# Seventeen homes for weight units and gathers of 192 one-hot columns in a grouped mixture of experts

## The reference, cut to what matters

```python
scores = sigmoid(t @ router_w)                 # t: (384, 1024), 16 experts
best = argmax(sum of the two best of each group of 4)   # group-limited
top_idx = top_k(where(mask, biased, -inf), 2); top_w normalised
g = einsum("nd,edf->nef", t, w_gate)           # (16, 1024, 1024) weights
u = einsum("nd,edf->nef", t, w_up)
a = silu(g) * u * combine
y = einsum("nef,efd->nd", a, w_down)
x = x + g2 * y                                  # then the final RMSNorm
```

## Time and profile before

| what | value |
|---|---|
| median of three runs (lowest, highest) | 836.02 us (828.83, 836.41) |
| profiled execution | 833.07 us |
| span of its instructions | 831.4 us |
| TensorE, matmul records | busy 746.8 us, 90% of the span |
| TensorE, weight loads | 412.1 us, 50% |
| VectorE | 311.8 us, 38% |
| ScalarE | 187.1 us, 22% |
| GpSimd | 43.3 us, 5% |
| moved by DMA | 261.05 MB, mean 314 GB/s |
| mean granted clock of TensorE | 0.948 |

### The profile page before, as it was taken

The page is one execution under the profiler, slowest core; times in us unless marked ns, Lnnn a source line. Parts: engine busy times, 40 slices in busy tenths (PEclk is TensorE's granted clock), DMA queues, the critical chain, the costliest instruction groups (busy, mean ns, idle before and its releaser), DMA issues.

```text
span 831.4 us, 22823 instructions
## 1 busy us (share of the span) xinstructions
PE 746.8 (90%) x9748; PEld 412.1 (50%) x9749; DVE 311.8 (38%) x802; ACT 187.1 (22%) x392; POOL 43.3 (5%) x102
## 2 busy tenths in 40 slices
PE   5699986788999988999998999999999999999862
PEld 5345553474644466553552654554544554555232
DVE  3898969997012266211210121211201211121138
ACT  3555340200022133021211122201201112221132
POOL 2000100000010001200000000000000000000000
PEclk9989999957999976999999999999999999999985
DMA  8910369820139992699999999999999999999981
GB/s 340 413 43 2 127 247 410 344 97 7 50 119 334 361 364 95 214 406 410 410 410 411 409 411 411 410 410 411 410 409 379 413 411 410 410 410 410 410 334 76
DMA packets 70027, 261.05 MB, mean 314 GB/s; under 512 B 10540, under 2 KB 10588, under 8 KB 65880
## 3 DMA queue, kind: packets, MB, share of 16 engines
q1 hardware_dynamic: 67832, 257.17, 78.5%
q0 software_dynamic: 1552, 2.99, 0.9%
q10 hardware_dynamic: 592, 0.14, 0.1%
HBM read 252.49 MB, written 9.17 MB: 315 GB/s over the span
## 4 chain that ended last, share of the span: by engine, by line
PE 59%; DVE 10%; DMA 7%; SPq 6%; issue 2%; ACT 1%; DVEq 0%; ACTq 0%
PE ps L1231 23%; PE ps L1238 11%; PE ps L1223 8%; PE ps L1137 7%; DMA ring<-in_moe_w_up 6%; SPq L414 5%; DVE sreg L1592 3%; PE ps L1197 3%; PE ps L1073 3%; DVE scan_t L1584 3%; DMA vreg<-y_scratch 2%; PE ps L1298 1%; SPq L420 1%; PE ps L1081 1%; PE ps L1277 1%
## 5 line engine op out<-in xcount | busy, mean ns | idle before, releaser
L1231 PE MATMUL ps<-ring,vreg 128*32 128x512 f32 x2240 | 245.7, 593 | 13.1 <-DMA ring<-in_moe_w_up 8.2
L1231 PEld LDWEIGHTS ps<-ring,vreg 128*32 128x32 f32 x2240 | 72.3, 110 | 179.4 <-issue 161.2
L1238 PE MATMUL ps<-ring,vreg 128*32 128x256 f32 x2240 | 125.9, 383 | 0.8 <-ACT vreg L816 0.8
L1769 DVE TENSOR_TENSOR vreg<-vreg,ps 128x256 f32<-128x256 f32 x48 | 17.3, 417 | 212.2 <-ACT vreg L811 212.2
L1238 PEld LDWEIGHTS ps<-ring,vreg 128*32 128x32 f32 x2240 | 71.8, 111 | 48.8 <-issue 2.8
L1223 PEld LDWEIGHTS ps<-vreg,sreg 128*128 128x128 f32 x720 | 82.7, 192 | 12.6 <-issue 12.6
L1223 PE MATMUL ps<-vreg,sreg 128*128 128x96 f32 x720 | 86.0, 276 | 0.0
L1787 DVE COPY vreg<-ps 32x256 f32<-32x256 f32 x90 | 38.1, 424 | 99.6 <-PE ps L1238 97.2
L833 ACT ACTIVATE vreg<-ps 32x256 f32<-32x256 f32 x90 | 33.6, 373 | 139.4 <-PE ps L1238 137.6
L1137 PE MATMUL ps<-ring 128*128 128x512 f32 x128 | 58.7, 617 | 1.4 <-issue 0.7
L811 ACT ACTIVATE vreg<-ps 128x256 f32<-128x256 f32 x48 | 15.0, 385 | 196.4 <-PE ps L1231 196.4
(11 more groups left out here) (295 smaller groups left out, 608.0 us busy)
## 6 DMA issues: line engine op xcount, KB each, us to landing
ring<-in_moe_w_down SPq DMA_DIRECT2D x128, 512.0 KB, 12.2
ring<-in_moe_w_gate SPq DMA_DIRECT2D x123, 512.0 KB, 13.2
ring<-in_moe_w_up SPq DMA_DIRECT2D x123, 512.0 KB, 14.4
ring<-in_w_ada SPq DMA_DIRECT2D x24, 1024.0 KB, 11.7
ring<-in_ssm_w_glu SPq DMA_DIRECT2D x8, 1024.0 KB, 13.0
ring<-in_ssm_w_in SPq DMA_DIRECT2D x8, 512.0 KB, 21.7
y_scratch<-sreg SPq DMA_DIRECT2D x6, 512.0 KB, 7.6
sreg<-ada_rows SPq DMA_DIRECT2D x4, 512.0 KB, 8.4
```

What stands on the lines that cost most here:

```text
L1231: last = pe.matmul(ps[t][32 * j:32 * j + 32, :], xgT[:, k, 32 * t:32 * t + 32], w[:, :, 256 * j:256 * j + 256], start=(k == 0), stop=(k == ...
L1238: last = pe.matmul(ps[3 + t // 2][32 * dj:32 * dj + 32, 256 * (t % 2):256 * (t % 2) + 256], aT[:, t, c2, 32 * j:32 * j + 32], ring[:, KT + ...
```

## The change

The five further homes serve the whole loop. `odd_unit` holds units 7 to 11 of every odd expert; those of even experts stay in the ring; units 0 to 6 (`SINGLE = 7`) have one home each for all. For every expert SP issues units 7 to 11 first, which wait for the expert two before, and then units 0 to 6, which wait for the expert before. VectorE's five copies are gone. Before the loop the five extra homes are filled with units 7 to 11 of expert 1.

Tokens are gathered in pairs. Expert 1 keeps a gather of its own with 96 columns (`gather_one`), in expert 0 after `gate_up`, and then TensorE waits for VectorE to empty it (`single_ev`). Experts 2i+2 and 2i+3 are gathered together by `pair_hot`, 192 columns: blocks k 0 to 3 during expert 2i and blocks 4 to 7 during expert 2i+1. The buffers of `load_y2` and of the final output move to the ring. The last expert's work on each engine keeps its order.

```diff
-            for u in range(len(early_unit), NU):
-                sp.wait_ge(unit_free, u + 1)
-                load_unit(u, 1)
-            with sp.Fori(2, NE) as e:
-                for u in range(NU):
-                    sp.wait_ge(unit_free, e * NU + (u + 1 - NU))
-                    load_unit(u, e)
+            def load_both(before, i, odd):
+                for u in range(SINGLE, NU):
+                    sp.wait_ge(unit_free, before + (int(odd) * NU + u + 1 - 2 * NU))
+                    load_unit(u, i, odd)
+                for u in range(SINGLE):
+                    sp.wait_ge(unit_free, before + (int(odd) * NU + u + 1 - NU))
+                    load_unit(u, i, odd)
+            for u in range(SINGLE):
+                sp.wait_ge(unit_free, u + 1)
+                load_unit(u, 0, True)
+            with sp.Fori(1, NE // 2) as i:
+                for odd in (False, True):
+                    load_both(i * (2 * NU), i, odd)
...
+            def gather_two(k0, end):
+                for k in range(k0, end):
+                    col = k % 2 * 2 * CAP
+                    for t in range(NT):
+                        last = pe.matmul(ps[5 + k % 4 // 2][:, col:col + 2 * CAP], h2[:, t, k * P:(k + 1) * P],
+                                         pair_hot[:, t, :], start=(t == 0), stop=(t == NT - 1))
+                if end % 4 == 0:
                     last.then_inc(xt_ps, 1)
...
-                with pe.If(e < NE - 1):
-                    gather_x(it + 1, 0, 5)
+                if not odd:
+                    with pe.If(i < 1):
+                        pe.wait_ge(oh_ready, r * (PAIRS + 1) + 2)
+                        gather_one()
+                        pe.wait_ge(single_ev, r * 2 + 2)
+                with pe.If(i < PAIRS - 1):
+                    if odd:
+                        pe.wait_ge(xt_ev, two * 2 + 6)
+                    else:
+                        pe.wait_ge(oh_ready, r * (PAIRS + 1) + i + 3)
+                    gather_two(4 * int(odd), 4 * int(odd) + 3)
...
-                with pe.If(e < NE - 1):
-                    gather_x(it + 1, 5, KT)
+                with pe.If(i < PAIRS - 1):
+                    gather_two(4 * int(odd) + 3, 4 * int(odd) + 4)
...
+            def evict_two(gathers, k0, used):
+                dve.wait_ge(xt_ps, gathers)
+                for b in range(2):
+                    k = k0 + 2 * b
+                    dve.wait_ge(unit_free, used + k + 2)
+                    cp(xgT[:, k:k + 2, :, :], ps[5 + b][:, 0:4 * CAP].rearrange("p (k e n) -> p k e n", k=2, e=2)
+                       ).then_inc(xt_ev, 1)
...
-            for u in range(len(early_unit)):
-                dve.wait_ge(ld_early[u], 32)
-                dve.wait_ge(unit_free, u + 1)
-                cp(ring[:, u, :], early_unit[u]).then_inc(ld_unit[u], 32)
-            with dve.Fori(0, NE - 2) as e:
-                expert(e, e + 2)
-            expert(NE - 2, None)
-            expert(NE - 1, None, True, True)
+            def odd_expert(it, gathers, units, pair=None):
+                evict_two(gathers + 3, 0, units)
+                products(it)
+                evict_two(gathers + 4, 4, units)
+                if pair is not None:
+                    find_pair(pair)
+                expert_rows(it)
+            even_expert(0, 2)
+            with dve.Fori(0, PAIRS - 2) as i:
+                odd_expert(i * 2 + 1, i * 2, i * (2 * NU) + NU, i * 2 + 4)
+                even_expert(i * 2 + 2)
+            odd_expert(NE - 3, NE - 4, NU * (NE - 3))
+            even_expert(NE - 2)
+            products(NE - 1)
+            expert_rows(NE - 1, True)
```

More of the change, by code:

```diff
@@ L458, in _ @@
             with sp.If(v > CAP):
+                sp.wait_ge(dve_pre, NT)
                 with sp.Fori(1, ROUNDS) as r:
[L460 to L463, removed]
+                    with sp.Fori(0, NE // 2) as i:
+                        for odd in (False, True):
+                            load_both(r * (NE * NU) + i * (2 * NU), i, odd)
                 sp.wait_ge(y_sent, 16 * NE * ROUNDS)
-                sp.wait_ge(dve_pre, NT)
                 load_y2()
@@ L1214, in _, with gather_one @@
                       start=False, stop=True, skip_group_check=True).then_inc(pe_pos, 1)
[L1216 to L1220, removed]
+            def gather_one():
+                for k in range(KT):
                     bank, col = (ps[5], k) if k < 5 else (ps[6], k - 5)
@@ L1255, in expert @@
-            def expert(it, e, count=None):
-                pe.wait_ge(xt_ev, it * 2 + 2)
+                        wait_unit(KT + kk // 2, it, two, odd)
+                    down(kk, 2, odd)
+            def expert(r, i, odd, count=None):
+                it = r * NE + i * 2 + int(odd) if count is None else i * 2 + int(odd)
+                two = r * NE + i * 2 if count is None else i * 2
+                pe.wait_ge(xt_ev, two * 2 + 4)
                 pe.wait_ge(prod_done, it * TT + TT)
                 if count is None:
-                    third_gate_up(it)
+                    third_gate_up(it, two, odd)
@@ L1317, in _ @@
                 last = pe.transpose(ps[3][0:CAP, t * P:(t + 1) * P], oh_last[:, t, :], ident[:])
[L1318 removed]
+            last.then_inc(pe_pos, 1)
             pe.wait_ge(dve_cmax, 1)
[L1320 to L1322 removed]
+            with pe.Fori(0, PAIRS) as i:
+                for odd in (False, True):
+                    n = pe.value_load(counts[0:1, bass.ds(i * 2 + int(odd), 1)], min_val=0, max_val=T)
+                    expert(0, i, odd, n)
             v = pe.value_load(cmaxi[0:1, 0:1], min_val=0, max_val=T)
@@ L1326, in _ @@
                     pe.wait_ge(xt_ev, r * (2 * NE))
-                    gather_x(r * NE, 0, KT)
-                    with pe.Fori(0, NE) as e:
-                        expert(r * NE + e, e)
+                    pe.wait_ge(oh_ready, r * (PAIRS + 1) + 1)
+                    gather_one()
+                    with pe.Fori(0, PAIRS) as i:
+                        for odd in (False, True):
+                            expert(r, i, odd)
                 pe.wait_ge(y_ev, 12 * NE * ROUNDS + 12)
@@ L1764, in other_choice, with products @@
                 tt(m, m, x1[:, t, :], ALU.add).then_inc(dve_pre, 1)
-            def expert(it, next_but_one, last_of_round=False, last=False):
+            def products(it):
                 for t in range(TT):
```

166 lines of the change are left out of this document (91 added, 75 removed).

## The result

| kernel | median | lowest, highest | profiled: time, span | granted clock |
|---|---|---|---|---|
| before | 836.02 us (5 runs) | 828.83, 836.75 | 833.07, 831.4 | 0.948 |
| after | 900.6 us (5 runs) | 893.8, 902.72 | 893.8, 892.1 | 0.914 |

The ratio is 1.0792, interval 1.0742 to 1.0842: slower by 8%, 62.6 us behind the forecast of 838.0 and far outside 830 to 845. The spans differ by 60.7 us. TensorE's loop over the experts starts 6.0 us earlier in the profiled execution after (320.21 against 326.24), so loop and tail together lose 66.7.

What follows compares the result with a forecast made beforehand. The prediction took the queue of weight transfers to bound the loop. Last landing 8.2 us earlier (-8.7 + 1.6 - 1.1) and a tail 10.4 us longer gave +2.2 us: 838 from 836.02, range 830 to 845.

Steps and rivals of the forecast that it cites:

- New branches on TensorE fall into its 3 to 5 us of slack per expert: TensorE's loop: added branches cost nothing, since each expert's transfers take 30.7 us and its TensorE work 27.4.
- The rest of the loop: After expert 0: transfers always find free homes, added waits cost nothing, and 1.1 us of queue idling goes.
- four rivals: Other outcomes: full end clock with cheaper gather (835), over 1% faster (0.11), clock low for good (0.09), head start lost (0.10).
- rival C: Last expert: the clock falls for good as `gate_up` starves for seven units; 9.1 us more, 847 us; chance 0.09.
- Head start (-8.7): Loop start: the next unit fetched waits for one used unit instead of six, so the queue restarts 8.7 us earlier.
- Expert 0 (+1.6): Expert 0: the gathers delay `down` by 5.6 us, so the queue idles 4.4 us instead of 2.8; 1.6 lost.
- idle time near 630: Mid-loop, behind an expert with a third group of slots: the queue's 1.1 us of idling disappears.
- W (-8.2): End of the loop: the last weights' landing, 800.7 us before, moves 8.2 us earlier; bounds -9.5 and -6.8.
- The 2.56 us: Weight queue: time to transfer one 1.05 MB unit at 410 GB/s, twelve units to an expert.
- The tail (+10.4): After the last landing: more work waits for the last unit, now unit 6, so the combine starts 10.4 us later.
- W': Landing of the last weights in the kernel after, forecast near 792.5; the combine was to start 25.6 us behind it.
- The sum: Whole kernel: earlier last landing (-8.2) and longer tail (+10.4) make +2.2 us, 838 on the median.

Runs made afterwards that it cites:

- b_pairloop: The kernel before with only TensorE's loop changed to take two experts per turn; 903.65 us, ratio 1.0842.
- b_pad4: The kernel before with four always-skipped blocks of 128 instructions added to TensorE's loop body (some 1430 in all); 848.18 us, ratio 1.0154.
- a_unrolled: The kernel after with TensorE's sixteen experts written out, no loop; 839.58 us, ratio 1.0054.
- a_nothird: The kernel after without the matmuls of any third group of slots (body some 1340, rows beyond 64 tokens wrong); 833.36 us, ratio 1.0014.
- a_unr_choices: The kernel after, TensorE's experts written out, with ScalarE scaling all tiles before the copies to `y_last`; 832.88 us, ratio 1.0016.
- b_unrolled: The kernel before with TensorE's sixteen experts written out, no loop; 841.2 us, ratio 1.0068.
- b_pad7: The kernel before with seven always-skipped blocks of 128 instructions in TensorE's loop body (some 1820 in all); 1162.17 us, ratio 1.3921.

## Why the prediction was wrong, and where it was right

**The step that failed** is "New branches on TensorE fall into its 3 to 5 us of slack per expert", under "The rest of the loop", where the queue was said to set the pace. It costed the new loop as branches at no price, and never counted the body: 876 matmul and load instructions became 1752, and seven jumps back stop for 70.2 us (10.0 each). `b_pairloop` shows that this alone makes the loss. The size could be counted in the kernel (the body contains `odd` in both values); the sign to ask by was the 40 packets of the instruction queue on the page before. None of the four rivals had it; rival C had a low clock, but in the last expert and for another reason.

**The slack was too large as well.** 3.3 us, the lower end of "3 to 5", hold in the kernel before for an expert of two groups (27.39 us against 30.7). The three long experts take 37.46 (449.61 to 488.39 in `b_pad4`, less 1.32), so the mean is (13 x 27.39 + 3 x 37.46) / 16 = 29.3: 1.4 us of slack. And TensorE starts with seventeen units in hand, so it has to wait even less: the 8.2 us in the earlier trace rows are all that `gate_up` waited for transfers in the whole loop, half a us per expert. That is why the 1.0 us more per expert and the one long stop of `b_pad4`, 1.7 us per expert together and well within "3 to 5", used it up: its experts follow each other at TensorE's pace (28.45 us), with no wait for a transfer.

**Head start (-8.7): right.** The first issue comes 2.0 us after the loop's start and not 10.6, in every form with the new order (325.31 after a start at 323.32 in `a_unrolled`).

**Expert 0 (+1.6): right.** `down` starts 6.0 us later (forecast 5.6, the wait for VectorE being 1.58 us), a 192-column matmul costs 0.34 us, and the queue idles: (0.52 + 0.96 + 0.79) x 2 = 4.5 us from 344 to 350 in the kernel after, against the forecast 4.4. The idle time near 630 is gone in `a_unrolled`.

**W (-8.2): too large.** From the loop's start to the last weights the kernel before took 474.5 us. `a_unrolled` takes 473.5, and `a_nothird`, without stops for code, 469.6: a gain of 1.0 and 4.9. The stops may account for part of the difference between the two. In `a_nothird`, whose jumps don't stop, two stretches can be told apart. At expert 4 it is 5.7 us ahead where 7.1 was forecast (41 units fetched 118.9 us after the loop's start, against 39 after 119.4). From there a unit takes 2.62 us (446.28 to 796.94, 134 units), against 2.61 before (445.61 to 790.13, 132 units), where the idle time near 630 is included. So the 1.1 us near 630 are lost again to a queue that is half a per cent slower, and why is not settled. The 2.56 us were too small in both kernels: the queue also carries GpSimd's rows, 2.99 MB on the page before (q0), which at 410 GB/s are some 0.5 us per expert, an estimate. One reading of the earlier trace rows was off, and nothing hangs on it: of the slices named as full, the 17th has 214 GB/s and the 39th 334.

**The tail (+10.4): right in mechanism, 2 us too long.** Every link is in the rows of `a_unrolled`. It runs W' + 23.6 and not 25.6; with the full clock, which the prediction gave as 23.9, it is 0.3 off. The clock stayed up there in spite of waits of 0.37 to 1.47 us for single units, and `a_unr_choices` had the low one (3.49 us for the first 32 of `down`).

**The sum**, for a TensorE that finds its code, was 838; `a_unrolled` measured 839.58. That these meet is partly luck. In the profiled executions it is 4.5 us longer than the kernel before (837.57 against 833.07): its loop starts 2.9 us earlier (323.32 against 326.24), W gains 1.0 us where 8.2 was forecast, and the tail costs 8.4 where 10.4 was. The start of the loop lies anywhere from 320.21 to 327.89 in these traces, which the prediction doesn't cover. So the head start, expert 0 and the links of the tail hold, the gain of W doesn't, and the term that wasn't worked out was over 60 us.

## What to carry to other kernels

When a change makes a loop body longer, count its instructions per engine, skipped branches too, before anything else: here bodies of up to some 1600 on TensorE, executed nearly whole, jumped back in 0.3 us, and 1850 cost 10 us a round. Idle time put down to "issue" at the top of a loop, with more packets on the instruction queue, is the sign, and taking the loop alone (or writing it out) tests it in one run. Slack is a mean over all rounds, long ones included, and an operation that relieves an engine off the bound earns nothing while it may delay the first round.

## What the hardware showed that was not expected

A jump back that misses costs 9.5 to 11.5 us in the kernel after (once 5.9), and a stop where TensorE runs straight on only 0.7 to 2.5 us (`a_unrolled`, `b_unrolled`). What sets the price is open. By the theory the code waits behind the weights, and in the kernel after the weight queue is indeed full during the stop. `b_pad7` shows that this can't be all of it. Windows of its stop from 403.6 to 425.56 (columns as above):

```profile
408.00:412.00 4.00, 0.00 (x0) 0.00 (x0) 0.00 (x0) 0.00 (x0) 0.32 (x1) 0.50 0.85 337
412.00:416.00 4.00, 0.00 (x0) 0.00 (x0) 0.00 (x0) 0.00 (x0) 0.37 (x2) 0.50 0.06 18
416.00:420.00 4.00, 0.00 (x0) 0.00 (x0) 0.00 (x0) 0.00 (x0) 0.00 (x0) 0.50 0.05 8
420.00:424.00 4.00, 0.00 (x0) 0.00 (x0) 0.00 (x0) 0.00 (x0) 0.00 (x0) 0.50 0.01 4
```

The weights have landed at about 412, and TensorE stands still for 13 us more with next to nothing being transferred. After such stops the granted clock is at 0.50, which costs 1.3 to 2.8 us more in the `gate_up` behind them (kernel after).

The Trainium skill, "Runtime: NRT & Kernel Launch", section "Instruction fetch mechanics", gives TensorE room for 2048 instructions, refilled in blocks of 256. In the next lines it speaks of a room of two blocks only (32 KiB, the size that it gives for most other engines), and says that a taken branch to code outside a window of two blocks stalls. The runs fit neither alone. A jump back over some 900 to 1600 instructions costs 0.3 us, so far more than two blocks stay; and at 1750 to 1850, below 2048, it misses. The section says that kernels prefer full unrolling where possible; the runs agree for the long loop (900.6 to 839.6 us) but not for the short one: the kernel before written out takes 841.2 us, 1.0068 of the loop's time (1.0037 to 1.0098).
